# A two-layer hybrid attention encoder: the query projections of the 1024-token request as three f16 products of scaled parts

## The reference

```python
h = rms_norm(x, g_norm) * (1 + scale) + shift
proj = h @ w_in            # q_lat 256 | kv | k_rope | z_a 512 | q_b 512 | k_b | v_b | z_b 512 columns
qa = rotate(rms_norm(q_lat, g_qa) @ w_uq)                 # 8 heads of 96
oa = softmax(qa @ ka.T * MLA_SCALE) @ va                  # group A, latent attention
ob = softmax(qb @ kb.T * GQA_SCALE) @ vb                  # group B, grouped queries
out = concat(oa * silu(z_a), ob * silu(z_b)) @ w_out
x = x + gate * out
```

## Time and profile before

| | us |
|---|---|
| median of 3 runs | 2523.54 |
| the 3 runs | 2521.19 to 2524.41 |
| the profiled execution | 2522.44 |
| span of its profile | 2520.6 |
| TensorE busy | 2317.3 (92%) |
| VectorE busy | 1315.5 (52%) |
| ACT busy | 920.3 (37%) |
| POOL busy | 772.6 (31%) |

### The profile page before, as it was taken

One profiled execution on the slowest core, in us unless ns is written; L12 is line 12 of the kernel. 1 busy time (PEld: TensorE's weight loads), 2 busy tenths in 40 slices (PEclk: granted clock), 3 DMA queues, 4 the chain that ended last, 5 costly groups with the idle time before them and its releaser, 6 DMA issues.

```text
span 2520.6 us, 43403 instructions
## 1 busy us (share of the span) xinstructions
PE 2317.3 (92%) x15914; PEld 1371.6 (54%) x15914; DVE 1315.5 (52%) x2252; ACT 920.3 (37%) x2130; POOL 772.6 (31%) x1277
## 2 busy tenths in 40 slices
PE   3888998889999999999988899989999999999997
PEld 1445544455656666666544455545556656665654
DVE  3545444555555555555644444546466455555563
ACT  0123323214444444444521333422344444444442
POOL 0553231554222122122127432146523113212210
PEclk7899999999999999999999999999999999999999
DMA  8711112220000000000422000143000000000001
GB/s 295 271 43 68 59 67 95 91 110 9 18 18 8 25 17 8 25 17 17 146 108 96 18 18 25 38 141 142 9 18 18 17 33 25 8 33 25 8 26 42
DMA packets 66694, 142.04 MB, mean 56 GB/s; under 512 B 7074, under 2 KB 31752, under 8 KB 66588
## 3 DMA queue, kind: packets, MB, share of 16 engines
q1 hardware_dynamic: 66592, 140.67, 15.8%
HBM read 115.44 MB, written 25.21 MB: 56 GB/s over the span
## 4 chain that ended last, share of the span: by engine, by line
PE 72%; DVE 15%; issue 5%; ACT 2%; SPq 2%; POOL 2%; DMA 2%; DVEq 0%; POOLq 0%; ACTq 0%
PE psum L621 56%; PE psum L611 9%; PE psum L824 6%; DVE region L1087 4%; DVE nmax L1070 3%; DVE hT L928 2%; ACT region L1243 1%; POOL region L1292 1%; DVE region L1045 1%; DVE KTa L888 1%; ACT region L1219 1%; DVE region L1047 1%; DVE region L1096 1%; DMA hT<-h_transposed 1%; PE psum L615 0%
## 5 line engine op out<-in xcount | busy, mean ns | idle before, releaser
L621 PE MATMUL psum<-Wq,hT 128*128 128x512 f32 (+1 forms) x1536 | 615.7, 548 | 18.8 <-DMA hT<-h_transposed 13.1
L1243 ACT ACTIVATE region<-psum 128x512 f16<-128x512 f32 x640 | 353.5, 594 | 761.6 <-PE psum L611 761.5
L1087 DVE TENSOR_TENSOR region<-psum,region 128x512 f16<-128x512 f32 x640 | 416.4, 684 | 309.1 <-ACT region L1243 308.2
L611 PE MATMUL psum<-ident,region 128*128 128x128 f32 (+1 forms) x3208 | 435.9, 277 | 23.0 <-DVE Va L984 7.9
L621 PEld LDWEIGHTS psum<-Wq,hT 128*128 128x128 f32 x1536 | 288.4, 193 | 264.3 <-issue 224.9
L1070 DVE TENSOR_REDUCE nmax<-psum 128x1 f32<-128x1024 f32 (+1 forms) x384 | 399.3, 1040 | 44.8 <-PE psum L621 43.8
L611 PEld LDWEIGHTS psum<-ident,region 128*128 128x128 f32 (+1 forms) x3208 | 356.6, 140 | 106.4 <-issue 79.4
L621 PE MATMUL psum<-Wout,region 128*128 128x512 f32 x768 | 353.3, 605 | 9.2 <-DVE region L1055 6.7
L621 PE MATMUL psum<-KTa,region 96*128 96x512 f32 x640 | 311.2, 601 | 18.6 <-DVE region L1045 12.9
L1292 POOL TENSOR_TENSOR rsum<-sums,v_scale 128x8 f32<-128x8 f32 x48 | 9.7, 203 | 831.0 <-ACT region L1235 831.0
L1292 POOL TENSOR_TENSOR region<-region,rope_sb 128x64 f32<-128x64 f32 (+3 forms) x384 | 158.2, 433 | 342.1 <-DVE region L1041 325.9
(11 more groups left out here) (110 smaller groups left out, 1930.8 us busy)
## 6 DMA issues: line engine op xcount, KB each, us to landing
Wout<-in_w_out SPq DMA_DIRECT2D x8, 2048.0 KB, 9.9
h_transposed<-hT SPq DMA_DIRECT2D x24, 512.0 KB, 2.6
Va<-in_w_ada SPq DMA_DIRECT2D x12, 1024.0 KB, 5.4
Wq<-in_w_in SPq DMA_DIRECT2D x6, 2048.0 KB, 14.2
hT<-h_transposed SPq DMA_DIRECT2D x24, 512.0 KB, 3.3
Wq<-in_w_ada SPq DMA_DIRECT2D x3, 2048.0 KB, 12.8
Wout<-in_w_ada SPq DMA_DIRECT2D x3, 2048.0 KB, 13.5
x_after_layer<-region SPq DMA_DIRECT2D x12, 512.0 KB, 2.6
```

Of the source, the lines that this page charges most:

```text
L611: return nc.tensor.transpose(out, in_, ident[0:n, 0:n])
L621: last = nc.tensor.matmul(out, lhsTs[k], rhss[k], start=k == 0, stop=k == n - 1)
L1087: nc.vector.tensor_tensor(PT[:, 1, pt_block(h, S, 4 * c):pt_block(h, S, 4 * c) + 4, :], psum[:, T_BANK + b, :].rearrange("p (c n) -> p c n ...
L1243: nc.scalar.activation(PT[:, 0, pt_block(h, S, 4 * c):pt_block(h, S, 4 * c) + 4, :], psum[:, T_BANK + b, :].rearrange("p (c n) -> p c n", ...
```

## The change

For the 1024-token request the query projections are no longer f32 products. The weights `Wq` and the modulated rows `hT` are each scaled by a power of two and cut into a high and a low f16 part; a k-block then takes three f16 matmuls (high by high, high by low, low by high) in place of one f32 matmul of two records. The 512-token request still multiplies in f32. The slots and the bank of the side products stay as they are.

- While the 512-token request of a layer is in its attention stretch, `Wq` is worked through in 14 chunks of 1024 elements a partition. In tile 1 VectorE takes the largest magnitude of one chunk at the end of each of the slots 0 to 13. POOL reduces over partitions, and VectorE makes the scales at slot 3 of tile 2. Then at 14 slots (tile 2: 4, 6, ... 14; tile 3: 0, 2, ... 14) ACT writes the high part of a chunk, VectorE the low part one slot later, and SP stores both parts into `w_kept` in DRAM.
- In the key steps of the 1024-token request ACT makes the high part of the rows (`h_high`) ahead of the next rows' square, VectorE the low part (`h_low`) at the end of the step, and SP stores the parts in place of `hT`, after `h_low`.
- In step 0 of these SP loads all weight parts into `Wq` (two DMAs, 7.3 MB together).
- Copies of q_lat and q_b become scalings; the scale of tanh and of the gates takes the rest: one more POOL operation on 8 columns for each half of a tile.
- For the 512-token passes the loop over the middle tiles is written out.

The core of the diff:

```diff
+W_CHUNKS = [(k, 4, Q_LAT, QR) for k in range(0, KD, 4)] \
+    + [(k, 2, c, MIX) for c in (Q_QB, Q_ZA, Q_ZB) for k in range(0, KD, 2)]
+W_TOP_TILE, W_SCALE_TILE, W_SCALE_SLOT = 1, 2, 3
+W_SPLIT_SLOTS = [(2, h) for h in range(4, 16, 2)] + [(3, h) for h in range(0, 16, 2)]
+assert len(W_SPLIT_SLOTS) == len(W_CHUNKS) <= 2 * HEADS - 2
...
-    h_kept = [nc.dram_tensor(f"h_transposed_{r}", (SEQS[r] // P, P, KD * P), F32, kind="Internal").ap() for r in range(2)]
+    h_kept = [nc.dram_tensor(f"h_transposed_{r}", (SEQS[r] // P, P, (1 + r) * KD * P), (F32, F16)[r], kind="Internal").ap()
+              for r in range(2)]
+    w_kept = [nc.dram_tensor(f"w_in_parts_{l}", (P, KD, 2 * QC), F16, kind="Internal").ap() for l in range(DEPTH)]
...
+        parts = sb("parts", [P, 2, 2 * D], F16)
...
+        hT_parts = hT[:, 0, :, :].rearrange("p k n -> p (k n)").bitcast(F16).rearrange("p (a k n) -> p a k n", a=2, k=KD)
+        Wq_parts = Wq[:, :, :].rearrange("p k n -> p (k n)").bitcast(F16).rearrange("p (k n) -> p k n", k=KD)
+
+        def w_chunk(j):
+            k, n, c, w = W_CHUNKS[j]
+            return Wq[:, k:k + n, c:c + w], parts[:, j % 2, :].rearrange("p (k a n) -> p k a n", k=n, a=2)
...
-            with tile_loop(eng, 1, NT - 1, **per) as i:
-                tile(i, False, False)
+            if NT == tiles[0]:
+                for i in range(1, NT - 1):
+                    tile(i, False, False)
...
+                if r:
+                    sp.wait_ge(s["h_low"], n)
+                    rows = parts[:, odd, :]
+                else:
+                    sp.wait_ge(s["mm_free"], n)
+                    rows = hT[:, odd, :, :].rearrange("p k n -> p (k n)")
+                sp.dma_start(h_kept[r][bass.ds(t, 1)].rearrange("o p n -> p (o n)"), rows) \
+                    .then_inc(s[f"h_stored{odd}"], 16)
+
+            def keep_w(j):
+                sp.wait_ge(s["w_low"], len(W_CHUNKS) * l + j + 1)
+                k, n, c, w = W_CHUNKS[j]
+                sp.dma_start(w_kept[l][:, k:k + n, 2 * c:2 * (c + w)], parts[:, j % 2, :].rearrange("p (k n) -> p k n", k=n)) \
+                    .then_inc(s[f"w_stored{j % 2}"], 16)
+
+            def load_w():
+                for j in (-2, -1):
+                    sp.wait_ge(s[f"w_stored{j % 2}"], w_stored(l, len(W_CHUNKS) + j))
+                for k in range(0, KD, KD // 2):
+                    sp.dma_start(Wq_parts[:, k:k + KD // 2, :], w_kept[l][:, k:k + KD // 2, :]).then_inc(s["w_parts_loaded"], 16)
...
+                if r:
+                    keep_h(r, 0, 0, kept_before[q] + 1)
                 key_step(0, 0)
+                if r:
+                    load_w()
...
+            def product3(out, low, high, half=""):
+
+                for k in range(KD // 2 if half == "1" else 0, KD // 2 if half == "0" else KD):
+                    nc.tensor.matmul(out, hT_parts[:, 0, k, :], high(k), start=k == 0, stop=False)
+                    nc.tensor.matmul(out, hT_parts[:, 0, k, :], low(k), start=False, stop=False)
+                    last = nc.tensor.matmul(out, hT_parts[:, 1, k, :], high(k), start=False, stop=k == KD - 1)
+                return last
...
-                        last = product(ps[:, 0:w], [hT[:, 0, k, :] for k in range(KD)],
-                                       [Wq[:, k, c0:c0 + w] for k in range(KD)], half)
+                        if r:
+                            if name == "q_lat" and isinstance(i, int) and i == 0:
+                                pe.wait_ge(s["w_parts_loaded"], 32 * (l + 1))
+                            last = product3(ps[:, 0:w], lambda k: Wq_parts[:, k, 2 * c0 + w:2 * (c0 + w)],
+                                            lambda k: Wq_parts[:, k, 2 * c0:2 * c0 + w], half)
+                        else:
+                            last = product(ps[:, 0:w], [hT[:, 0, k, :] for k in range(KD)],
+                                           [Wq[:, k, c0:c0 + w] for k in range(KD)], half)
...
-                if c == 0:
+                if c == 0 and m % 2 == 0:
...
+                def query_weights(i, h):
+
+                    if i == W_TOP_TILE and h < len(W_CHUNKS):
+                        ins = nc.vector.tensor_reduce(w_top[:, h:h + 1], w_chunk(h)[0], AX_XY, ALU.max, apply_absolute_value=True)
+                        if h == len(W_CHUNKS) - 1:
+                            then(ins)
+                    if i == W_TOP_TILE and h == len(W_CHUNKS):
+                        nc.vector.tensor_reduce(w_max[:, l:l + 1], w_top[:, :], AX_X, ALU.max).then_inc(s["w_top_local"], 1)
+                    if (i, h) == (W_SCALE_TILE, W_SCALE_SLOT):
+                        input_scales()
+                    if (i, h - 1) in W_SPLIT_SLOTS:
+                        j = W_SPLIT_SLOTS.index((i, h - 1))
+                        dve.wait_ge(s["w_high"], len(W_CHUNKS) * l + j + 1)
+                        w, out = w_chunk(j)
+                        nc.vector.scalar_tensor_tensor(out=out[:, :, 1, :], in0=w, scalar=in_scale[:, l, 1:2], in1=out[:, :, 0, :],
+                                                       op0=ALU.mult, op1=ALU.subtract).then_inc(s["w_low"], 1)
+
+                def h_low(t, odd):
+
+                    dve.wait_ge(s["h_high"], kept_before[q] + t + 1)
+                    nc.vector.scalar_tensor_tensor(out=parts[:, odd, D:2 * D], in0=hT[:, odd, :, :].rearrange("p k n -> p (k n)"),
+                                                   scalar=in_scale[:, l, 0:1], in1=parts[:, odd, 0:D],
+                                                   op0=ALU.mult, op1=ALU.subtract).then_inc(s["h_low"], 1)
...
+                    if r and (not isinstance(i, int) or i + 1 < NT):
+                        h_low(i + 1, 1 - odd)
...
+                            if r and (not isinstance(t, int) or t + 1 < NT):
+                                h_high(t + 1, 1 - odd, at[name] + key_names(i, NT).index("h^T1"))
...
+                def h_high(t, odd, n):
+
+                    act.wait_ge(s["mm_free"], n)
+                    wait(act, f"h_stored{odd}", 8 * (b0 + t - odd))
+                    if isinstance(t, int) and t < 2:
+                        act.wait_ge(s[f"w_stored{odd}"], w_stored(l, len(W_CHUNKS) - 2 + odd))
+                        act.wait_ge(s["in_scales"], l + 1)
+                    nc.scalar.activation(parts[:, odd, 0:D], hT[:, odd, :, :].rearrange("p k n -> p (k n)"), ACT.Copy,
+                                         scale=in_scale[:, l, 0:1]).then_inc(s["h_high"], 1)
+
+                def query_weights(i, h):
+
+                    if (i, h) in W_SPLIT_SLOTS:
+                        j = W_SPLIT_SLOTS.index((i, h))
+                        if j < 2:
+                            act.wait_ge(s["in_scales"], l + 1)
+                            wait(act, f"h_stored{j}", 8 * b0)
+                        wait(act, f"w_stored{j % 2}", w_stored(l, j - 2))
+                        w, out = w_chunk(j)
+                        nc.scalar.activation(out[:, :, 0, :], w, ACT.Copy, scale=in_scale[:, l, 1:2]).then_inc(s["w_high"], 1)
...
+                    if r:
+                        then(mul(inv, inv, in_unscale[:, l, 0:1].broadcast_to([P, HEADS])))
...
+                        if r == 0 and (i, h) == (W_SCALE_TILE, 0):
+                            pool.wait_ge(s["w_top_local"], l + 1)
+                            nc.gpsimd.partition_all_reduce(w_max[:, l:l + 1], w_max[:, l:l + 1], P, RMAX) \
+                                .then_inc(s["w_top_ready"], 1)
```

More of the change, by code:

```diff
@@ L142, in encoder @@
     trounds = [t // 4 for t in tiles]
+    kept_before = [0, 0, tiles[1], tiles[1]]
     tr_before = [sum(16 * tiles[p] * trounds[p] for p in range(q)) for q in range(len(inst))]
@@ L348, in over_tiles @@
             tile(0, True, False)
-            with tile_loop(eng, 1, NT - 1, **per) as i:
-                tile(i, False, False)
+            if NT == tiles[0]:
+                for i in range(1, NT - 1):
+                    tile(i, False, False)
+            else:
+                with tile_loop(eng, 1, NT - 1, **per) as i:
+                    tile(i, False, False)
             tile(NT - 1, False, True)
@@ L571, in tile @@
                             side(name, owner(name, i))
+                        if r == 0 and (i, h - 1) in W_SPLIT_SLOTS:
+                            keep_w(W_SPLIT_SLOTS.index((i, h - 1)))
                 tile(0, True, False)
-                with tile_loop(sp, 1, NT - 2, rounds=(rounds, PER_SIDE + (len(ADA) if q == 0 else 0))) as i:
-                    tile(i, False, False)
+                if r == 0:
+                    for i in range(1, NT - 2):
+                        tile(i, False, False)
+                else:
+                  with tile_loop(sp, 1, NT - 2, rounds=(rounds, PER_SIDE + (len(ADA) if q == 0 else 0))) as i:
+                      tile(i, False, False)
                 tile(NT - 2, False, False)
@@ L979, in value_scales, with input_scales @@
```

(19 more changed lines are left out.)

41 lines of the change are left out of this document (30 added, 11 removed).

## The result

The changed kernel took 2550.0 us (median of 4 runs, 2545.0 to 2556.6), the kernel before 2523.5 beside it: ratio 1.0107, 95% interval 1.0087 to 1.0127. It is slower by 26 us, where 35 less was forecast, and above the whole range. The profiled execution took 2556.6 us (span 2554.8).

What follows compares the result with a forecast made beforehand. TensorE was taken to bound the 1024-token attention stretches. Terms -95 + 27 + 29 + 4 = -35 took the profiled 2522.4 us to 2487, shown as a median of 2488 us; 8-in-10 range 2455 to 2515.

Steps and rivals of the forecast that it cites:

- TensorE, -95: 1024-token attention: half products and q_lat as f16 matmuls save 6.1 us a tile over sixteen tiles; 95 us less, bounds 85 to 97.
- The 512-token passes, +27: Reductions and high and low parts there, 100 us of work, mostly hidden; 13.5 us show per pass, bounds 12 to 45.
- The weight load, +29: Key step 0: 7.34 MB queued ahead of tile 3's rows idles TensorE and slows its clock; 14.5 us per pass, bounds 26 to 60.
- the other edits, +4: Row parts in key steps, layer 1's start, POOL's added operation, stores, written-out loops: 4 us together, bounds 1 to 10.
- Written-out loops: Among the small edits: writing out loops was to cost nothing, as no wait stands at a loop's end.
- the slower one, preparation not hidden: Rival: all 100 us of reductions and parts show in the 512-token passes, 2561 us, deciding from 62 on; chance 0.04.

Runs made afterwards that it cites:

- the kernel padded by 30: The changed kernel plus 60 satisfied waits, joined to 30 instructions, at the start of TensorE's program: 2501.5 us, ratio 0.9916 to the kernel before.

## Why the prediction was wrong

Against the kernel padded by 30, whose profiled execution is 24 us below before, the terms can be read without the gap.

- **TensorE, -95: right.** Half a product took 2.59 us; a tile of layer 0 fell from 91.65 to 85.74. The attention stretches gave 43.7 and 40.1, and the stretch behind the last kv product of each long pass 6.9 and 2.5 more: 93.2. The 12 loads add nothing to that. By the rule that I had weighed against this (the Trainium skill, TensorE: Matmul & The Clock Gate, section Part 3, The mechanism) they would not hide, and the trace disagrees: 2.59 us for twelve pairs is 0.216 each, what the pairs of before took. The same section also lets a load into the background weight buffer go ahead of matmuls under way, which I had left out; no row here shows that buffer.
- **The 512-token passes, +27: too low, 10 us under what was measured.** Measured 17.0 and 19.9, together 36.9 (within the bounds of 12 to 45). The durations were right (reduction 1.21, low part 1.28, high part 1.15 us), tile 1 cost 5.0 and 6.4 for 4, tile 2 4.5 and 3.9 for 5; the last tile 7.6 and 9.5 for 4.5. The 4.5 were for its light slots alone, 2 to 8, and these grew by 4.2 and 5.2, as counted. The rest lies where I had counted nothing: 1.2 in slot 1 in each layer, and 1.6 and 3.2 from slot 13 to the end.
- **The weight load, +29, and the other edits, +4: right.** Over the key steps the long passes grew by 15.1 and 15.9 us: the late step took 24.4 and 22.0 instead of 10, the first two of layer 1 1.4 and 2.4 longer, where parts of the rows were added. Together 31 against 33; the queue goes in order, as the earlier trace rows had it.
- **The step that failed** is among the other edits: "Written-out loops: nothing, no wait stands at a loop's end." I had looked for waits that the written-out loops could add. What they change is the position of everything behind them, and the longer body changes where its end falls. In layer 1 it fell where the body is fetched anew at each jump, and five jumps cost some 9 us each: 44.9 in that attention stretch, of 48.5 between the medians. No view of before shows such a gap, but the row of the instruction queue was on its page (65 packets, and none from 860 to 1210 us, inside layer 0's loop), and I did not read it.

Without the gap, -93 + 37 + 31 + 1 (the rest) is -24., 11 less than forecast, nearly all of it the 512-token passes; the padded kernel's median of 2501.5 is within the range and 13 above the forecast. With the gap, the kernel is on the other side of no change. None of the rivals was this one: the slower one, preparation not hidden, did not come; 37 of 100 us show, and it decided from 62.

## What to carry to other kernels

Where a change lengthens a loop body or writes a loop out, look at the instruction packets of the page and at "issue" gaps at the loop's first instruction; the time of unchanged code can move by tens of microseconds for its position alone, so a gain or loss of a per cent is only the edit's own once a few instructions of padding leave it as it is. Large loads belong in pieces behind the small ones that are wanted soon, and away from the end of a stretch, where something else is wanted. Work that is put into another engine's idle time is hidden where the bounding engine has a product of its own to run, but not all of it even there: count every slot that gets some. In the light slots here 4.2 and 5.2 of 7.3 us showed.

## What the runs showed of the hardware that was not expected

- A packet of the instruction queue is 16 KB and holds 256 TensorE instructions here. A loop of 6.2 such blocks stays loaded over five jumps, with one packet or none fetched inside it, or is fetched anew at each: the branch takes 3.3 to 4.5 us instead of 0.21, TensorE is idle for 6.0 to 7.4 us, and the jump costs some 9 us in all; 30 instructions ahead of it decide.
- The clock falls with a single gap: within 6.93 us of idle time the granted clock fell from 1.00 to 0.50, and it stayed at 0.50 for the next 6 us, with TensorE busy all of them.
- Code that runs straight on for 131 packets costs nothing that these runs could see.
